# 31 chunk transposes of a fused transformer kernel: from TensorE to VectorE blocks and ScalarE copies

## The reference

```python
# first block: attention, then feed-forward
x = x + sliding_window_attention(rms_norm(x, mixer_norm), ...)
x = x + (silu(h @ w_gate) * (h @ w_up)) @ w_down          # h = rms_norm(x, ffn_norm)
# second block, layer 0: chunkwise mLSTM mixer with 8 heads
h = modulate(rmsnorm(x, g_pre), shift, scale)
proj = h @ w_in                                            # q,k | v | o | z | gates
qk = silu(causal_conv(proj[..., :A_V0], conv_w, conv_b))   # 4 taps along the rows
ht = mlstm_chunkwise(q, k, v, li, lf)                      # decay matrix, stabilised
y = sigmoid(o) * rmsnorm(ht, g_head) * silu(z)
x = x + gate * rmsnorm(y @ w_out, g_post)
# second block, layer 1: keys and values from x, chunk-band attention with 16 heads
k_sh, v_sh = (modulate(rmsnorm(x, kv_g), ...) @ kv_w)
o = chunk_band_attention(q, k_sh, v_sh, rel_table)
x = x + gate * rmsnorm((o * silu(z)) @ w_out, g_post)
```

## Time and profile before

| | before |
|---|---|
| median of 3 runs | 2426.06 us (2425.93 to 2426.3) |
| profiled execution, span | 2424.4 us |
| PE busy | 2408.2 us, 99% |
| DVE busy | 1726.8 us, 71% |
| ACT busy | 1170.0 us, 48% |
| granted TensorE clock | 0.999 |
| DMA, mean | 238 GB/s |

### The profile page before, as it was taken

How to read it: one execution, slowest core, us unless ns; L and a number is a source line. 1 busy time by engine, 2 the same in 40 slices (tenths; PEclk the granted TensorE clock), 3 DMA queues, 4 the chain that set the end, 5 groups by cost and what they waited for, 6 DMA issues and landing times.

```text
span 2424.4 us, 31019 instructions
## 1 busy us (share of the span) xinstructions
PE 2408.2 (99%) x11417; PEld 1960.0 (81%) x11417; DVE 1726.8 (71%) x2422; ACT 1170.0 (48%) x1583; POOL 45.2 (2%) x65
## 2 busy tenths in 40 slices
PE   9999999999999999999999999999999999999998
PEld 7778888888888888778888888888888778888887
DVE  8885777777777776667778667677676676667665
ACT  6665444444444444554444434444444564455553
POOL 1100000000000000000000000000000000000000
PEclk9999999999999999999999999999999999999999
DMA  8445888888888887567777787767777467776654
GB/s 299 141 136 175 265 292 294 307 294 293 284 296 292 291 297 228 163 225 237 241 232 234 239 265 244 237 231 235 240 232 240 156 193 255 242 238 212 232 192 139
DMA packets 161829, 578.16 MB, mean 238 GB/s; under 512 B 18288, under 2 KB 20592, under 8 KB 161680
## 3 DMA queue, kind: packets, MB, share of 16 engines
q1 hardware_dynamic: 160432, 572.64, 71.3%
q0 software_dynamic: 1104, 3.28, 0.4%
q10 hardware_dynamic: 144, 0.26, 0.0%
HBM read 574.01 MB, written 2.10 MB: 238 GB/s over the span
## 4 chain that ended last, share of the span: by engine, by line
PE 96%; DVE 2%; ACT 1%; DMA 1%; issue 0%; POOL 0%; SPq 0%; DVEq 0%; ACTq 0%
PE PS L1177 30%; PE PS L1179 30%; PE PS L1178 30%; PE PS L796 1%; DVE WL L2165 1%; PE PS L908 1%; DMA X<-in_x 0%; ACT WH L1552 0%; PE PS L803 0%; PE PS L876 0%; DVE X L2132 0%; PE PS L1004 0%; PE PS L1078 0%; PE PS L1024 0%; PE PS L1021 0%
## 5 line engine op out<-in xcount | busy, mean ns | idle before, releaser
L2165 DVE TENSOR_TENSOR WL<-W,WH 128x1024 fp32r<-128x1024 f32 x814 | 991.2, 1224 | 528.6 <-ACT WH L1552 526.0
L1552 ACT ACTIVATE WH<-W 128x1024 fp32r<-128x1024 f32 x814 | 857.4, 1060 | 923.0 <-PE PS L1179 912.6
L1177 PE MATMUL PS<-WH,XTH 128*128 128x512 f32 x2144 | 855.3, 399 | 3.6 <-DVE XTL L1683 1.2
L1179 PE MATMUL PS<-WH,XTL 128*128 128x512 f32 x2144 | 835.9, 390 | 0.0
L1178 PE MATMUL PS<-WL,XTH 128*128 128x512 f32 x2144 | 835.0, 389 | 0.0
L1177 PEld LDWEIGHTS PS<-WH,XTH 128*128 128x128 f32 x2144 | 402.6, 188 | 94.5 <-issue 10.1
L1179 PEld LDWEIGHTS PS<-WH,XTL 128*128 128x128 f32 x2144 | 402.3, 188 | 85.7
L1178 PEld LDWEIGHTS PS<-WL,XTH 128*128 128x128 f32 x2144 | 402.9, 188 | 83.6 <-issue 3.8
L1177 PE MATMUL PS<-WH,YTH 128*128 128x512 f32 x1120 | 441.0, 394 | 2.5 <-DVE WL L2165 1.8
L1179 PE MATMUL PS<-WH,YTL 128*128 128x512 f32 x1120 | 436.2, 389 | 0.0
L1178 PE MATMUL PS<-WL,YTH 128*128 128x512 f32 x1120 | 436.1, 389 | 0.0
(11 more groups left out here) (282 smaller groups left out, 1171.3 us busy)
## 6 DMA issues: line engine op xcount, KB each, us to landing
W<-in_vec SPq DMA_DIRECT2D x192, 512.0 KB, 4.6
W<-in_avoz SPq DMA_DIRECT2D x192, 512.0 KB, 4.5
W<-in_wg SPq DMA_DIRECT2D x88, 512.0 KB, 4.7
W<-in_wu SPq DMA_DIRECT2D x88, 512.0 KB, 4.9
W<-in_wd SPq DMA_DIRECT2D x88, 512.0 KB, 4.7
W<-in_gate SPq DMA_DIRECT2D x64, 512.0 KB, 4.4
W<-in_aqk SPq DMA_DIRECT2D x64, 512.0 KB, 4.4
W<-in_aout SPq DMA_DIRECT2D x64, 512.0 KB, 4.3
```

What stands on the lines that cost most here:

```text
L1177: e.matmul(p, x, WH[:, g % NH, j], start=first, stop=False)
L1179: i = e.matmul(p, y, WH[:, g % NH, j], start=False, stop=last)
L1552: e.activation(WH[:, n % NH], W[:, i % NW], ACT.Copy).then_inc(s_hi, 1)
L2165: e.tensor_tensor(l, src, h.bitcast(F32), ALU.subtract).then_inc(s_lo, 1)
```

## The change

`blocks_T` has DVE transpose the 32 x 32 blocks of a chunk in place of the block grid (two instructions of 128 x 512, one per 128 rows, into `TQ`); `quadrants` has ACT put the blocks where they belong (16 copies of 32 partitions x 256 elements, from `TQ` into the new buffer `MT`, or into `KT` for keys), two copies per tick, four in the last feed-forward chunk. `pairs_T` and `pair_lows` then make the upper and lower parts from `MT` instead of PSUM. This replaces the PE transposes of 11 feed-forward chunks, 8 mixer results, 4 key chunks and 8 query/key chunks of the mixer.

In `mix` the steps move back: conv from T5 to T11, `SG` and `QM` from T10 to T16, the query-key product from T16 to T21, denominator and numerator by 5 ticks, `G1` stays where it was. `weave` leaves out eight places behind the first gate weights, so that the V items start about 14 slots later and stand a little closer. The scratch for dynamic DMA is 8192.

```diff
-    e1 = rows_later(gate(VGT0) + vector(VSH0) + vector(VSC0) + vector(VSHK))
+    e1 = rows_later(gate(VGT0) + [("-",)] * 8 + vector(VSH0) + vector(VSC0) + vector(VSHK))
...
 # PE, ffn
-                yield from ticks(5)
-                banks = [take(("mid", f, a)) for a in range(2)]
-                w.wait_ge(s_mid, 2 * f + 2)
-                turns_by_rows(banks, MID)
...
 # PE, mix
-                yield from ticks(4)
-                for half in range(2):
-                    b, full = take(("qkT", h, half))
...
-                    four_turns(b, lambda j, t: QK[:, t, 128 * (2 * half + j):128 * (2 * half + j) + 128], full)
...
+                yield from ticks(10)
                 b, full = take(("decay", h))
...
-                yield from ticks(6)
+                yield from ticks(11)
                 b, full = take(("qk", h))
...
 # ACT, new
+            def quadrants(number, dst, n, sem):
+                w.wait_ge(s_tq, number)
+                for x in range(16):
+                    a, b = slice(32 * (x // 4), 32 * (x // 4) + 32), x % 4
+                    o = dst[32 * b:32 * b + 32].rearrange("p j (t r) -> p t j r", t=2)[:, :, :, a]
+                    i = e.activation(o, TQ[a].rearrange("p t (j b r) -> p t j b r", j=4, b=4)[:, :, :, b], ACT.Copy)
...
+                    if x % n == n - 1:
+                        yield
...
 # ACT, ffn
-                yield from ticks(21)
-                for half in range(2):
-                    w.wait_ge(s_unit, free)
-                    halves_T(("mid", f, half), 4 * slot, None)
-                    yield
+                yield from ticks(19)
+                yield from quadrants(TQ_FFN + f + 1, MT, 4 if f == 10 else 2, s_mt)
+                w.wait_ge(s_unit, free)
+                yield from pairs_T(MT_FFN + f + 1, 4 * slot, None)
...
 # ACT, mix
-                yield from ticks(10)
+                yield from ticks(3)
+                yield from quadrants(TQ_MIX + 2 * h + 1, MT, 2, s_mt)
+                yield from ticks(5)
                 w.wait_ge(s_mix, at("cvb"))
...
 # DVE, new
+            def blocks_T(src):
+                for t in range(2):
+                    i = e.transpose(TQ[:, t], src[:, t])
...
 # DVE, mix
-                    b = full(("qkT", h, half))
+                    w.wait_ge(s_mt, MT_MIX + 2 * h + 1)
...
-                yield from ticks(5)
+                yield
+                w.wait_ge(s_mixa, ata("qk"))
+                w.wait_ge(s_mix, at("qk"))
+                yield from blocks_T(QK)
+                yield from ticks(8)
                 conv(0, 0)
```

More of the change, by code:

```diff
@@ L1032, in mix, with to_T @@
                 gfree[ends[3][0]] = [(s_mix, at("z0")), (s_mix, at("z1"))]
[L1033 to L1041, removed]
+                yield
+            def to_T(j):
                 yield from ticks(4)
-                banks = [take((key, n, a)) for a in range(2)]
-                w.wait_ge(s_qc0, n + 1)
-                w.wait_ge(s_qc1, n + 1)
+                banks = [take(("qT", j, a)) for a in range(2)]
+                w.wait_ge(s_qc0, 4 + j + 1)
+                w.wait_ge(s_qc1, 4 + j + 1)
                 turns_by_rows(banks, QC)
                 for a in range(2):
-                    give((key, n, a), s_kq, 2 * n + a + 1)
+                    give(("qT", j, a), s_kq, 4 + 2 * j + a + 1)
                     yield
@@ L1435, in mix @@
                 e.activation(SG[:, 512:1024], Gb[ends[3][0]][1][:, :], ACT.Sigmoid).then_inc(s_mixa, 1)
[L1436 to L1455, removed]
+                yield from ticks(5)
+                yield from quadrants(TQ_MIX + 2 * h + 2, MT, 2, s_mt)
+                base = CGH + 4 * h - 4 * (h % 4)
+                w.wait_ge(s_unit, free)
+                yield from pairs_T(MT_MIX + 2 * h + 2, 4 * (h % 4), lambda kt: cols[:, base + kt:base + kt + 1])
             def qc(n, par, g):
                 w.wait_ge(s_unit, g)
-                if n:
-                    w.wait_ge(*filled(("kT" if n <= 4 else "qT", n - 1, 0)))
-                    w.wait_ge(*filled(("kT" if n <= 4 else "qT", n - 1, 1)))
+                if n > 4:
+                    w.wait_ge(*filled(("qT", n - 5, 0)))
+                    w.wait_ge(*filled(("qT", n - 5, 1)))
+                elif n:
+                    w.wait_ge(s_kq, n)
                 e.activation(QC[:, 0], Gb[par][0][:, :], ACT.Copy).then_inc(s_qc0, 1)
@@ L1465, in keys @@
                 qc(j, par, g)
-                yield from to_T("kT", j, KT[:, 4 * j:4 * j + 4])
+                yield from ticks(3 if j else 16)
+                w.wait_ge(s_post, 8)
+                yield from quadrants(TQ_KEYS + j + 1, KT[:, 4 * j:4 * j + 4], 2, s_kq)
             def values(j, par, g):
@@ L1487, in band @@
                 qc(4 + j, par, g)
-                yield from to_T("qT", 4 + j, Q4)
+                yield from ticks(4)
+                for half in range(2):
+                    b = full(("qT", j, half))
+                    if j:
+                        w.wait_ge(*filled(("bs", 4 * j - 1)))
+                    e.activation(half_rows(Q4, 0, 4, half), bank_rows(b, 0, 4), ACT.Copy).then_inc(s_kq, 1)
+                    yield
                 def score_(hh):
@@ L1888, in ffn @@
                     if f:
[L1889 to L1890 removed]
+                        w.wait_ge(s_mt, MT_FFN + f)
                     e.scalar_tensor_tensor(out=MID[:, t], in0=Gb[par][t][:, :], scalar=rst[:, t:t + 1],
                                            in1=SGT[:, t], op0=ALU.mult, op1=ALU.mult).then_inc(s_mid, 1)
[L1893 to L1896 removed]
+                yield
+                w.wait_ge(s_mid, 2 * f + 2)
+                yield from blocks_T(MID)
+                yield from ticks(5 if f == 10 else 9)
+                yield from pair_lows(4 * slot, None)
             def gate_w(g):
@@ L1989, in mix @@
                 step(e.reciprocal(rr1, d1))
-                yield from ticks(3)
+                yield from ticks(4)
                 settle()
```

96 lines of the change are left out of this document (63 added, 33 removed).

## The result

The changed kernel takes 2430.96 us in the median (2427.68 to 2433.59), the kernel before 2426.24 (2425.49 to 2427.67), on the same chip. The ratio is 1.0018, with a 95% interval of 1.0011 to 1.0025. I had forecast 2399.0 us. The profiled spans say the same: 2430.3 against 2424.4 us, 5.9 us more where the sum had 27.1 less. So 33.0 us are to be found (31.8 by the medians). The profiled execution is one of the slower ones: of the 20, the three with a granted clock of 0.994, this one among them, took 2432.8 to 2433.6 us, and the five with 0.996 took 2427.7 to 2428.6.

What follows compares the result with a forecast made beforehand. PE bounds the kernel, ACT and DVE having some 5.8 us in hand. From 2426.06 us, 27.1 (26.6 for transposes, 0.5 for the row of `c`) goes, the added work hidden: 2399.0 us, range 2396.4 to 2406.

Steps and rivals of the forecast that it cites:

- What goes: PE transposes removed: 23 groups at 0.85 us, 19.5 us, plus 7.2 us for query/key chunks; together 26.6 us.
- What comes: Added work: 496 ACT copies of 0.42 us, 208 us; 62 DVE block transposes of 0.7 us, 43 us.
- The step p: Spacing of ACT's small copies in a row: taken as 0.31 us, bounds 0.31 and 0.63.
- 10.7 + 16p, or +15.7: Start of a head: `MT` ready 15.7 us after the chunk's end, just in time for the convolution at +15.8.
- The margin of 1.65 us: Fourth head: time from `QM`'s end (+29.3) to PE's product (+30.95), down from 3.4 us.
- The first rival: Mixer waits for `QM`, 16p - 6.8 us in four heads: nothing to p = 0.42, 2404 at 0.5, 2415 at 0.6; 14%.
- The rival *slower: ACT copies alone make the kernel slower: p = 0.70 us cancels the gain, 0.75 gives 2432 us; chance 3%.
- The granted clock has nothing to fall from: PE's clock over the kernel: stays at its level because PE's gaps get fewer; no loss counted.
- The first head, "I count it at nothing": First mixer head, with the gates' steps and its convolution now behind them: no change in time counted.
- The last feed-forward chunk, "1.5 late": Four copies a tick there: ACT has 6.9 us of work in 5.4, 1.5 late; lower parts still precede the down projection.
- loads as a limit: Feed-forward rival: about 300 GB/s at DMA share 0.88 limits it, 9.4 us lost, 2408 us; chance 5%.
- the row of `c`: V items 14 slots later: PE's 0.45 us loss at ACT's wait for this broadcast row goes, 0.5 us gained.

Runs made afterwards that it cites:

- blocks together and product later: Changed kernel with both block transposes of each pair in one step, convolutions in place, sigmoid, `QM` and product three steps later: 2400.13 us, 0.9893.
- the wait filled: Changed kernel with matmuls of ones, overwritten by the product, put before PE's wait for `QM` in heads 1 to 7: 2423.52 us, 0.9990.
- the blocks together: Changed kernel with both block transposes of every pair in one schedule step, no weight tile or V item between them: 2410.87 us, 0.9937.
- the copies in place: Changed kernel with all 496 copies writing to the partitions of their input, so the result is not the reference's: 2408.78 us, 0.9928.
- With the product later: Changed kernel with only the query/key product and what follows it in the head four schedule steps later: 2427.82 us, 1.0005.

## Why the prediction was wrong

- **What goes** was right: 0.85 us for each feed-forward group. Of the 27 us nearly all arrive in the run with blocks together and product later (profiled span 2398.5, 25.9 less than before).
- **What comes** was right in duration. The step p was not: 0.425 us and not 0.31. I took the overlap from copies of full weight tiles, each in the same partitions as the one before. The small copies do stand 0.31 us apart under that condition, but in the change each one writes to another group. The figure that I set aside, 0.40, "if none of it overlapped", was the better one. The Trainium skill ("VectorE: DVE Perf Modes", section on the TRN2 errata) gives it, with 224 cycles for each instruction; the trace has 415 ns for its 400.
- **The step that failed** is the chain at the start of a head, `MT` at "10.7 + 16p, or +15.7". Its first number was wrong by more than p: I began the chain where ACT and VectorE stood before the change and did not add to them what the change itself puts just ahead of it, the previous head's result copies (2.5 us), and I priced the four weight tiles between the small copies at 0.945 us where they take their full 1.06 and more (0.6 us). With p = 0.425 in my own formula, `MT` would be at +17.5 and no head would wait (16p - 6.8 = 0.0); by the trace it is +20.6. The margin of 1.65 us became a wait of 3.3 us.
- **The first rival** named the right place and put the wrong price on it: "nothing up to p = 0.42". The waits are 17.7 us at p = 0.425. The rival *slower* asked for p = 0.70, and the kernel is slower at 0.425: neither had the chain's late start in it.
- **"The granted clock has nothing to fall from"** failed. It fell to the 1.2 GHz level in the four heads with stands of 3.05 us and more. By their timelines the product took 2.58, 2.58, 2.53 and 2.16 us from its first matmul to the next big one, where the heads with shorter stands have 1.33: 4.5 us. The big matmuls behind it lost another 1.2, 1.6, 0.5 and 0.8 us: 4.1. The run with the wait filled got 7.4 us back by the medians, 9.0 by the profiled spans, where these sum to 8.6. Behind the first head's stand seven steps of 0.43 us cost another 1.4. "TensorE: Matmul & The Clock Gate" of the Trainium skill (Part 1, the HAM clock gate) says that the hardware gates the clock by how busy PE is; the filled wait is this case's evidence for it.
- **The first head, "I count it at nothing"**: 3.5 us of wait at L967 against 0.3 before, 3.2 us.
- **The last feed-forward chunk, "1.5 late", no loss**: PE lost 1.3 us there. With the blocks together it lost nothing, and with the copies in place neither. So it took both, ScalarE's stand for the second transpose (3.57 us at 911.86) and the step of 0.425.
- **Not wrong**: loads as a limit (0.85 share, 292 GB/s; ScalarE's 41.6 us of waits for them cost PE nothing before the last feed-forward chunk, in which ScalarE waits for none), the row of `c` (0.6 us), ACT's next weight tile behind `QM`.

The account: 17.7 for the waits for `QM`, 3.2 in the first head, 1.3 in the last chunk, 8.6 + 1.4 = 10.0 for the slow clock; together 32.2 of 33.0 us. Of the rest, the product behind even a short stand takes 1.33 us and not 1.22, seven times 0.1.

## What to carry to other kernels

When a change adds work to an engine in stretches that repeat, start the sum of each chain from where the engine will stand after the added work of the stretch before, and follow every queue in which an instruction waits with others behind it: a stand of 5 us on ScalarE appeared in no wait of PE. Two instructions that produce one result belong together in the queue. When a late chain is put right, move the wait that blocks a queue and the consumer, and leave the steps whose data is there where they are; and price a PE wait of 3 us at more than 3 us (here 1.6 to 2.9 us more for each of the four before the product).

## What the runs showed of the hardware

- ScalarE copies of 32 partitions x 256 elements, SBUF to SBUF: 0.415 us each. In a row they begin 0.425 us apart when each writes to another group of 32 partitions than the one before, 0.31 to 0.32 when input and output stay in the partitions of the copy before, 0.41 from one such group to the next.
- VectorE's 32x32 block transpose of 128 x 512 float32: 0.702 us.
- PE's granted clock: after the five stands of 3.05 to 3.9 us of the changed kernel (four for `QM`, one in the first head) matmuls ran at the lower level for up to 6 us (1333.5 to 1340). Of the shorter stands most were followed by full speed, but not all. Of the two of 2.8 us with both blocks together, one slowed the product (2.58 us) and one didn't (1.33). With the product later, one of 1.95 us was followed by eight steps of 0.41 to 0.43 us and one of 2.16 us by none. So the length of a stand alone doesn't tell.
